# RWKV turns with the input slabs in a fifth place, loaded through ScalarE's own DMA queue, and with time budgets on TensorE

## The reference

```
z = h @ w_in;  za, zb, zc = split(z)                 # 47 tiles of 128 columns
oa = dilated_attention(za); ob = spatial_gating(zb)
oc = rwkv7_time_mix(zc)      # r, k, v, decay, a, g; scan over tokens; group norm
x = x + rmsnorm(concat([oa, ob, oc]) @ w_out)
x = x + rmsnorm(memory_cross_attention(...)); x = x + rmsnorm(conv_ffn(...))
# second block, two layers:
shift, scale, gate = split(silu(c) @ w_mod[l] + b_mod[l])   # the "modulation"
hl = xl * (1 + scale) + shift;  xl = layernorm(ALPHA * xl + gate * mixed(hl))
```

## Time and profile before

| what | us |
|---|---|
| median of three runs (3490.88 to 3493.23) | 3493.11 |
| the profiled execution, whole | 3494.48 |
| its span on the core | 3492.7 |
| TensorE busy in the span | 3160.5 (90%) |
| the six turns, from the first L739 to the next stage's first matmul | 185.55 to 740.61 |

### The profile page before, as it was taken

One profiled execution on the slowest core, in us unless ns is written; L12 is line 12 of the kernel. 1 busy time (PEld: TensorE's weight loads), 2 busy tenths in 40 slices (PEclk: granted clock), 3 DMA queues, 4 the chain that ended last, 5 costly groups with the idle time before them and its releaser, 6 DMA issues.

```text
span 3492.7 us, 51745 instructions
## 1 busy us (share of the span) xinstructions
PE 3160.5 (90%) x21160; PEld 2713.8 (78%) x21160; DVE 1619.7 (46%) x2569; ACT 1271.0 (36%) x1889; POOL 17.4 (0%) x33
## 2 busy tenths in 40 slices
PE   6978888867986899999999899999998968999997
PEld 6945555545985899999999688778887848889886
DVE  4333333334551655565544532455464356236755
ACT  3311111125433454444433422444443223236542
POOL 0000000000000000000000000000000000000000
PEclk8999888887997999999999999999999979999998
DMA  7555566541541355555455322222223213224342
GB/s 219 182 206 226 207 241 241 223 181 35 182 141 52 121 180 180 181 181 179 160 177 179 127 96 97 74 84 92 78 83 135 96 48 121 86 105 145 139 152 108
DMA packets 73115, 501.12 MB, mean 143 GB/s; under 512 B 8332, under 2 KB 8460, under 8 KB 20112
## 3 DMA queue, kind: packets, MB, share of 16 engines
q1 hardware_dynamic: 69264, 477.69, 37.8%
q0 software_dynamic: 3712, 21.40, 1.9%
HBM read 492.50 MB, written 6.55 MB: 143 GB/s over the span
## 4 chain that ended last, share of the span: by engine, by line
PE 81%; DVE 8%; DMA 5%; ACT 4%; issue 2%; SPq 0%; DVEq 0%; ACTq 0%
PE bank L653 41%; PE bank L972 7%; PE bank L709 6%; DMA ring_f<-in_w_in 5%; PE bank L1003 5%; PE bank L1005 5%; PE bank L1004 5%; DVE ring_f32r L1529 2%; PE bank L718 1%; PE bank L772 1%; ACT high_f32r L1137 1%; DVE x_f L1526 1%; PE bank L585 1%; PE bank L1035 1%; PE bank L947 1%
## 5 line engine op out<-in xcount | busy, mean ns | idle before, releaser
L1529 DVE TENSOR_TENSOR ring_f32r<-ring_f,high_f32r 128x1024 fp32r<-128x1024 f32 (+1 forms) x692 | 780.1, 1159 | 810.0 <-ACT high_f32r L1137 808.9
L653 PE MATMUL bank<-y_f32r,high_f32r 128*128 128x256 f32 (+1 forms) x3168 | 980.0, 309 | 52.9 <-DVE h_f32r L1529 31.0
L1137 ACT CAST high_f32r<-ring_f 128x1024 fp32r<-128x1024 f32 (+1 forms) x692 | 655.7, 997 | 960.7 <-PE bank L653 666.1
L653 PE MATMUL bank<-h_f32r,high_f32r 128*128 128x256 f32 (+1 forms) x2400 | 757.1, 315 | 0.9 <-DVE ring_f32r L1529 0.9
L653 PE MATMUL bank<-y_f32r,ring_f32r 128*128 128x256 f32 (+1 forms) x2464 | 749.2, 304 | 0.0
L653 PEld LDWEIGHTS bank<-y_f32r,high_f32r 128*128 128x128 f32 x3168 | 611.7, 193 | 83.1 <-issue 46.0
L653 PEld LDWEIGHTS bank<-y_f32r,ring_f32r 128*128 128x128 f32 x2464 | 477.2, 194 | 17.0
L653 PEld LDWEIGHTS bank<-h_f32r,high_f32r 128*128 128x128 f32 x2400 | 463.1, 193 | 28.1 <-DVE ring_f32r L1529 1.3
L653 PE MATMUL bank<-z_f32r,high_f32r 128*128 128x256 f32 x912 | 262.0, 287 | 10.3 <-DVE h_f32r L1529 7.4
L709 PE MATMUL bank<-h_f,ring_f 128*128 128x256 f32 x768 | 218.6, 431 | 15.9 <-DMA ring_f<-in_w_in 15.8
L1003 PE MATMUL bank<-h_f32r,high_f32r 128*128 128x512 f32 x512 | 209.3, 409 | 0.0
(11 more groups left out here) (397 smaller groups left out, 4489.1 us busy)
## 6 DMA issues: line engine op xcount, KB each, us to landing
ring_f<-in_w_in SPq DMA_DIRECT2D x159, 1024.0 KB, 4.8
ring_f<-in_w_mod SPq DMA_DIRECT2D x96, 1024.0 KB, 7.7
ring_f<-in_w_up SPq DMA_DIRECT2D x88, 1024.0 KB, 4.8
ring_f<-in_w_out SPq DMA_DIRECT2D x48, 1024.0 KB, 4.8
ring_f<-in_w_down SPq DMA_DIRECT2D x64, 704.0 KB, 4.1
ring_f<-in_w_kv SPq DMA_DIRECT2D x8, 1024.0 KB, 4.8
x_f<-in_ctxT POOLq DMA_DIRECT2D x2, 2048.0 KB, 11.7
ring_f<-in_w_q SPq DMA_DIRECT2D x4, 1024.0 KB, 4.8
```

Of the source, the lines that this page charges most:

```text
L653: last = mm(bk[(t0 + j) % banks][:, 0:width], w[:, c], x[:, k], start=(k == 0 and w is hi and x is rhs.hi), stop=(k == KC - 1 and w is lo))
L1137: act.copy(w_hi[p % 2][:, half], slot[s % SLOTS][:, half]).then_inc(w_high, 1)
L1529: return v.tensor_tensor(out, in0, in1, op)
```

## The change

- **A fifth place.** The second place of `high` is not in use during the turns but for two small buffers (`rz`); these now share the first, and the second becomes `slot_in`, the one place for the turn's input slabs.
- **ScalarE loads it.** `input_slab(n, i)` is issued on ScalarE's own DMA queue right behind the copy `beside1(m, i)` of the tile before, since only then has the place been read; the first one ahead of the turns. SyncE's four places hold modulation slabs only.
- **The order** of a turn is four modulation slabs, then an input tile, four times.
- **Time budgets.** A step of `projection1` tells its length, 0.434 us for a k and 0.87 us for a modulation slab, and `beside1(us)` takes steps until the time owed is used up. The budgets are 2.4, 6.5, 3.4, nine times 0.85 or 1.4, 0.85, 1.0, seven times 0.7 or 0.8, 1.4, and, new, 1.1 between the two matmuls of the group norm; the rest of the turn's steps follow.
- **The end of the modulation** is turned after k = 9 of input tile 3, not after it.
- **No copy of the up weights**: TensorE reads them where they lie; its turn starts on `gn_var` of the turn before.
- **ScalarE**: tile 1 is copied behind `rw_tz` (before: ahead of `rw_turned`); the group norm's square root comes before tile 2; the last turn is written out after a loop of five.
- **VectorE**: scan, `rw_cs` and `rw_bonus` go ahead of the wait for `rw_kkn`.

```diff
-TURN = [("in1", 0)] + [("mod", k) for k in range(5)] + [("in1", 1)] + ... + [("in1", 3)]
+TURN = [piece for m in range(4) for piece in [("mod", 4 * m + k) for k in range(4)] + [("in1", m)]]
+IN1_US, MOD_US = 0.434, 0.87
...
+        slot_in = arena[:, HI_AT + SLOT:HI_AT + 2 * SLOT]
-        rz = Area(HI_AT, 2 * SLOT)
+        rz = Area(HI_AT, SLOT)
...
             with sp.Fori(0, 5) as i:
...
+                for n in range(16):
+                    sp.wait_ge(S("mod_read"), i * 16 + (16 + n - SLOTS + 1))
+                    modulation_slab(n, i + 1)
...
                     if kind == "in1":
                         bank = bk[(23 + n) % 2]
+                        pe.wait_ge(S("w_in_extra"), (i * 4 + n + 1) * 16)
                         pe.wait_ge(gemm_free, i * 4 + (23 + n - 1))
                         for k in range(KC):
-                            last = mm(bank[:, 0:T], at_slot[:, k * P:(k + 1) * P], H[0][:, k, :],
+                            last = mm(bank[:, 0:T], slot_in[:, k * P:(k + 1) * P], H[0][:, k, :],
...
+                            if n == 3 and k == 9:
+                                pe.wait_ge(S("mod_row"), i + 1)
...
+                owed = 0.0
+                def beside1(us):
+                    nonlocal owed
+                    owed += us
+                    while owed > 0:
+                        owed -= next(pieces)
+                if i:
+                    pe.wait_ge(S("gn_var"), i)
-                pe.wait_ge(S("rw_up"), i + 1)
-                pe.wait_ge(S("rw_banks"), i + 1)
...
                 def evacuated(dve, act=None):
-                    beside1(2)
+                    beside1(1.4 if dve == 10 else 0.85)
...
+            def input_slab(n, i):
+                k = i * 4 + (23 + n)
...
+                act.dma_start(slot_in, src).then_inc(S("w_in_extra"), 16)
-                act.copy(upg, at(ups, i)).then_inc(S("rw_up"), 1)
...
                 beside1(0, i)
+                if loads > 0:
+                    input_slab(0 + 1, i)
...
-                beside1(1, i)
                 act.wait_ge(S("rw_turned"), i + 1)
...
                 last.then_inc(S("rw_tz"), 1)
+                beside1(1, i)
+                if loads > 1:
+                    input_slab(1 + 1, i)
+                act.wait_ge(S("gn_var"), i + 1)
+                f(rinv, rinv, ACT.Sqrt).then_inc(S("gn_std"), 1)
                 beside1(2, i)
+                if loads > 2:
+                    input_slab(2 + 1, i)
                 act.wait_ge(S("mod_read"), i * 16 + 16)
                 act.copy(mod_row, bk[7][:, :]).then_inc(S("mod_row"), 1)
-                act.wait_ge(S("gn_var"), i + 1)
-                f(rinv, rinv, ACT.Sqrt).then_inc(S("gn_std"), 1)
                 beside1(3, i)
+                if loads > 3:
+                    input_slab(3 + 1, i)
```

More of the change, by code:

```diff
@@ L446, in used, with modulation_slab @@
                         return gemm_done, TILE0[name] + tile, {"wo": 16, "down": 1}.get(name, 4)
[L448 to L460, removed]
+            def modulation_slab(n, i):
+                k = i * 16 + n
+                src = d["w_mod"][k, :, :] if isinstance(k, int) else d["w_mod"][bass.ds(k, 1), :, :].rearrange("a p n -> p (a n)")
+                sp.dma_start(slot[(23 + n) % SLOTS], src).then_inc(w_in_slot[(23 + n) % SLOTS], 16)
             for k in range(23):
@@ L465, in _ @@
                 sp.dma_start(slot[k % SLOTS], d["w_in"][k, :, :]).then_inc(w_in_slot[k % SLOTS], 16)
[L466 to L469, removed]
[L470 to L478 removed]
+            for n in range(16):
+                if n < SLOTS:
+                    sp.wait_ge(gemm_done, 23 - SLOTS + n + 1)
+                else:
+                    sp.wait_ge(S("mod_read"), n - SLOTS + 1)
+                modulation_slab(n, 0)
+            with sp.Fori(0, 5) as i:
+                for n in range(16):
+                    sp.wait_ge(S("mod_read"), i * 16 + (16 + n - SLOTS + 1))
+                    modulation_slab(n, i + 1)
             for name, nt, ns in STAGES[1:]:
@@ L712, in projection1 @@
                                 last.then_inc(gemm_done, 1)
-                            yield
-                    else:
+                            yield IN1_US
+                            if n == 3 and k == 9:
+                                pe.wait_ge(S("mod_row"), i + 1)
+                                for b in range(4):
+                                    last = mm(bk[7][:, 8 * b:8 * b + 8], mod_row[:, b * P:(b + 1) * P], mod_sel,
+                                              start=True, stop=True)
+                                last.then_inc(S("mod_turned"), 1)
+                    else:
+                        at_slot, done = slot[(23 + n) % SLOTS], w_in_slot[(23 + n) % SLOTS]
+                        pe.wait_ge(done, (i * 4 + ((23 + n) // SLOTS + 1)) * 16)
                         if n == 0:
@@ L720, in projection1 @@
                         last.then_inc(S("mod_read"), 1)
-                        yield
-                pe.wait_ge(S("mod_row"), i + 1)
-                for b in range(4):
-                    last = mm(bk[7][:, 8 * b:8 * b + 8], mod_row[:, b * P:(b + 1) * P], mod_sel, start=True, stop=True)
-                last.then_inc(S("mod_turned"), 1)
-                yield
+                        yield MOD_US
             pe.wait_ge(S("rw_lora"), 1)
@@ L1219, in _, with turn @@
             act.sem_inc(S("mod_out"), 1)
-            with act.Fori(0, C_TILES) as i:
-                act.copy(upg, at(ups, i)).then_inc(S("rw_up"), 1)
+            def input_slab(n, i):
+                k = i * 4 + (23 + n)
+                src = d["w_in"][k, :, :] if isinstance(k, int) else d["w_in"][bass.ds(k, 1), :, :].rearrange("a p n -> p (a n)")
+                act.dma_start(slot_in, src).then_inc(S("w_in_extra"), 16)
+            input_slab(0, 0)
+            def turn(i, loads):
                 act.wait_ge(S("rw_upmm"), i + 1)
```

59 lines of the change are left out of this document (25 added, 34 removed).

## The result

| what | before | after |
|---|---|---|
| median of the runs (lowest to highest), us | 3491.99 (3489.43 to 3493.23) | 3356.6 (3354.49 to 3357.46) |
| span of the profiled execution | 3492.7 | 3355.6 |
| first up matmul | 185.55 | 182.89 |
| a turn, first up matmul to the next | 91.2 to 95.7, mean 93.0 | 69.0 to 69.4, the first 71.05 |
| next stage's first matmul | 740.61 | 604.64 |

The ratio is 0.9612, with a 95% interval of 0.9596 to 0.9629: 135 us less, where 88 were forecast. The whole gain lies in the turns: the next stage starts 136.0 us earlier, 2.7 of which the first up matmul had already.

The account below looks back on a forecast made before the run. TensorE was taken as the bound, by its work and where it stands still. Per turn 69 work + 5.0 waits + 3.5 clock = 77.5 us, the next stage 87.9 us earlier, so 3405 us; range 3357 to 3453.

Parts of the forecast that it names:

- The waits for the fifth place: TensorE's waits for input slabs at tiles 0 to 3 of a turn: 1.6 to 6.6 us in sum, 5.0 taken.
- the shared value: Upper bound for an input slab's load, with a modulation slab sharing the engines all the while: 4.8 + 2.5 = 7.3 us.
- The walk: The new turn stepped through at full clock from its first up matmul, without a wait for slabs: 67.3 us.
- the median of 7.7: Median us to landing of slabs queued in the turns before the change, cited beside the load bounds 4.8 and 7.3.
- The clock: Time a turn loses to TensorE at 1.2 GHz behind waits, mainly tile 3's: bounds 1 and 7 us, 3.5 taken.
- the first rival: In the turns, loads aren't shared and the clock stays up: waits 1.6, 70 us a turn, 3360; chance 0.17.
- The work: TensorE's own work at full clock in a turn: trace leaves 68 to 71 us, 69 taken.
- The positions: Times in the turn when tiles are wanted: tile 1 at 21.0, tile 2 at 43.9, tile 3 at 62.2 us.
- The small parts: Turn starts, group norm, inversion steps, issues and the end: `upg`'s 2.4 us gone, third inversion step up to 0.4.
- The second: Rival: some 16 inversion and chain steps wait 0.3 us each for VectorE and ScalarE; 85 us a turn, 3450; chance 0.2.
- The third: Rival: TensorE's clock stays at 1.2 GHz for a share of the turn, slower from 0.28; at 0.4, 3540; chance 0.04.
- The fourth: Rival: input loads on ScalarE's queue wait behind `rw_tz` and the square root; 92 us a turn, no change; chance 0.02.

## Why the prediction was wrong

The direction held, and so did the account of where the gain comes from; three terms of one sum were all too large, by 8.3 us a turn together (77.5 against 69.2 = 67.4 + 1.6 + 0.2 at the inversion). The six turns took 600.78 - 182.89 = 417.9 us where 465 were forecast.

- **The waits for the fifth place, 5.0 forecast, 1.6 measured.** The step that failed is "so I take nearly the shared value". The walk put 3.2 us between the issue of slab 3 and its being wanted, and the trace 3.3 (379.70 to 383.00). The load itself took 4.9 and not 7: it goes out 0.95 us ahead of SyncE's slabs, and the run with both issued together shows that this lead is what spares it. The shared value was taken as if it didn't matter who comes first, and the median of 7.7 as that of any load, though it is that of loads queued behind others. Tiles 1 and 2 never wait, at the lower bound as well. Only in the sixth turn did tile 0 wait, 1.0 us: its slab took 6.7 us, the longest of the 24, and why is open.
- **The clock, 3.5 forecast, nothing measured in turns 2 to 5.** "Of the new waits only tile 3's is long" was right. That its first k would then take 0.9 us, as at 577.67, was not: behind 1.60 us they take 0.46. Where the clock did fall at this same place, behind waits of 5.1 to 8.8 us in two of the experiments, the k behind it cost 1.3 us or more, 2.3 behind 8.24: the price was of the right size, and what failed is that the wait would bring it. So the two terms were tied: with the wait the clock's term had to fall too, which is what the first rival did and the sum did not. Whether the 3.7 us of waiting that were forecast would have brought the clock down, no run shows; none has a wait between 1.8 and 5.1 us at tile 3. Only the first turn lost anything, 1.9 us: it starts behind a wait of 7.9 us, at 0.50 up to 187.
- **The work, 69 forecast, 67.4 measured.** The walk gave 67.3. I raised it because the trace left 68 to 71, with 7 to 10 us of clock taken off; the true loss was 77.8 - 67.4 = 10.4, and 92.2 - 14.3 - 10.4 = 67.5. The mean clock (10.1) had it, the reading stretch by stretch did not, since it counted only the runs of k that stood out.
- **The positions held up to tile 2** (21.0 forecast, 21.1 measured; 43.9 and 43.8) and were some 2.3 late at tile 3, both for its issue (59.0 and 56.6) and for its being wanted (62.2 and 59.9), so that the wait was not touched. With the 8.0 behind it 62.2 gives 70.2, not the walk's own 67.3: the total was right and this position wrong.
- **The small parts held.** `rw_ops` is level: L751 starts at 12.0 and VectorE ended at 11.6 (333.90 + 0.76), where 11.9 and 11.4 were forecast; no wait. The third inversion step waits 0.2 us, forecast up to 0.4. The first turn starts at 182.89 (183.6), and from the end of the last k to the next stage's first matmul it is 604.64 - 600.78 = 3.9 us (4.1). ScalarE's issues cost 0.34 (0.33). Modulation slabs are not waited for.
- **The rivals.** The numbers of the first, loads not shared and the clock up, came: 70 us a turn forecast, 69.2 measured. It had 0.17. Its mechanism came by half: loads issued together do share, and this one is spared by its lead. The objection to it, that four slabs ahead of tile 3 look like what came before each fall of the clock, is answered by the same place in the trace: 3.64 us of slabs, a wait of 1.6, then full clock. The second did not come: VectorE's answers fit. The third, a clock that stays low, did not come either; the nearest to it is the run with four waits of 2.8 to 5.0 us a turn, where the clock's share was 12.2 of the 95 us, less than the rival needed (0.28 x 65 = 18). The fourth, loads held up behind ScalarE's own waits, cost 0.1 us at slab 3 and no wait at slab 2.

Of what was won, a queue of its own gives nothing, no copy about 16 us (measured alone), VectorE's order 4 by the trace and nothing that the runs can tell, the budgets 19 to 21, and the rest, some 95, is the order and the fifth place together with ScalarE's order and the earlier turning, which no run takes apart. These don't add up exactly, as the single parts were measured beside different neighbours.

## What to carry to other kernels

When TensorE waits for slabs that come in bursts, give each kind of slab a place of its own and an order in which a burst is no longer than the ring; who issued the loads made no difference here. Issue the load that is wanted soonest first, be it by a microsecond: ahead it took 4.9 us here, together with another 8.2, behind another 9.7. Price waits and clock together, at both ends of the range, and take the clock's loss from the busy time and the mean clock, not from the rows that stand out.

## What the runs showed of the hardware

- A 1 MB load that is issued 0.95 us ahead of the first on another queue lands as if alone (4.9 us), though four follow: the other queue moves nothing for 2.9 us. At a lead of 0.05 both take 8.2 to 8.3 and move side by side, and 0.82 behind it takes 9.7. Which queue doesn't matter (3356.3 by one issuer, 3356.6 by two).
- The same 669 or 670 matmul records of a turn are busy 67.4 us at a granted clock of 1.00, 72.9 at 0.94, 77.8 at 0.87 and 79.6 at 0.84.
- A stretch of 16.3 us that is busy throughout, with the chain's small matmuls, ran at 0.50 behind a wait of 3.96 us; behind 5.01 us, with a row of k, the clock was back after 4.2 us. A single wait of 1.89 us at tile 0 of the fourth turn cost 1.7 us of clock in one run, and 1.84 us at the same place none in another.
